# Seven block products in all four feed-forwards of a two-layer streaming encoder, with their additions on GpSimd

## What is computed

```python
for l in range(DEPTH):                       # 2 layers
    u = rmsnorm(x, norm1[l]) @ w_in[l]       # D_MODEL 1024 -> heads A, B and C
    # A: differential attention; B: attention over the best 256 (sample: 136) keys of an
    # index score per frame; C: gated linear recurrence; then one output projection
    x = x + merge_heads(...) @ w_out[l]
    a, gate = split(rmsnorm(x, norm2[l]) @ w_up[l])      # 1024 -> 2 x 2816
    conv = b_conv + sum(ext[:, j:j + t] * w_conv[j] for j in range(3))   # ext = history, a
    x = x + (silu(conv) * gate) @ w_down[l]
y = rmsnorm(x, final_norm)
```

## Time and profile before

| | us |
|---|---|
| median of 3 runs | 4004.64 |
| profiled execution | 4004.88 |
| its span | 4003.0 |
| TensorE busy | 3717.8 |
| VectorE busy | 2334.5 |
| ScalarE busy | 1125.3 |
| GpSimd busy | 758.4 |
| mean granted TensorE clock | 0.964 of full |

### The profile page before, as it was taken

How to read it: one execution, slowest core, us unless ns; L and a number is a source line. 1 busy time by engine, 2 the same in 40 slices (tenths; PEclk the granted TensorE clock), 3 DMA queues, 4 the chain that set the end, 5 groups by cost and what they waited for, 6 DMA issues and landing times. The chain is left out here.

```text
span 4003.0 us, 54393 instructions
## 1 busy us (share of the span) xinstructions
PE 3717.8 (93%) x21676; PEld 2953.6 (74%) x21676; DVE 2334.5 (58%) x4713; ACT 1125.3 (28%) x2668; POOL 758.4 (19%) x812
## 2 busy tenths in 40 slices
PE   7978899999999999999899989999899999899998
PEld 5755678777877777777667877787767777688887
DVE  1663556599964553549546454289955655544542
ACT  1123333211134442321334233111134443312221
POOL 2200121201001032221000014313010001353344
PEclk9988899999999999999999999999999999899999
DMA  4322233412222132342221213333221122242223
GB/s 141 96 76 75 81 98 89 129 67 70 79 67 68 51 96 93 90 124 89 62 91 54 80 59 96 115 110 122 70 69 52 42 75 69 70 149 83 65 89 96
DMA packets 152757, 339.54 MB, mean 85 GB/s; under 512 B 30312, under 2 KB 70824, under 8 KB 139192
## 3 DMA queue, kind: packets, MB, share of 16 engines
q1 hardware_dynamic: 92728, 291.04, 23.3%
q10 hardware_dynamic: 59776, 45.02, 3.9%
HBM read 299.33 MB, written 36.68 MB: 84 GB/s over the span
## 5 line engine op out<-in xcount | busy, mean ns | idle before, releaser
L835 PE MATMUL PS<-xn,wring 128*128 128x272 f32 (+1 forms) x7168 | 1709.1, 398 | 73.1 <-ACT dense L1163 29.2
L835 PEld LDWEIGHTS PS<-xn,wring 128*128 128x128 f32 x7168 | 1387.1, 196 | 348.1 <-issue 48.7
L1776 POOL TENSOR_TENSOR xT<-xT,res 128x272 f32<-128x272 f32 (+1 forms) x320 | 252.6, 790 | 2391.9 <-ACT res L1118 2356.6
L835 PE MATMUL PS<-dense,wring 128*128 128x256 f32 (+1 forms) x2816 | 666.1, 395 | 17.8 <-DVE dense L1436 9.2
L835 PEld LDWEIGHTS PS<-dense,wring 128*128 128x128 f32 x2816 | 541.6, 195 | 118.4 <-issue 10.7
L1545 DVE MAX8 top<-scr 128x8 f32<-128x384 f32 (+6 forms) x418 | 367.4, 879 | 12.5
L1546 DVE MATCH_REPLACE8 scr<-top,scr 128x384 f32<-128x384 f32 (+6 forms) x418 | 359.8, 861 | 0.0
L1118 ACT ACTIVATE res<-PS 128x272 f32<-128x272 f32 (+1 forms) x320 | 123.9, 389 | 600.5 <-PE PS L835 576.4
L856 PE MATMUL PS<-wring,xn 128*128 128x256 f32 (+1 forms) x1152 | 266.0, 391 | 3.7 <-ACT dense L1132 3.7
L856 PEld LDWEIGHTS PS<-wring,xn 128*128 128x128 f32 (+1 forms) x1152 | 213.3, 187 | 50.0 <-ACT dense L1132 5.4
L835 PE MATMUL PS<-catT,wring 128*128 128x272 f32 (+1 forms) x1024 | 231.1, 387 | 2.5 <-DVE catT L1615 1.8
(11 more groups left out here) (196 smaller groups left out, 4127.5 us busy)
## 6 DMA issues: line engine op xcount, KB each, us to landing
wring<-in_wu SPq DMA_DIRECT2D x88, 1024.0 KB, 4.8
wring<-in_wf SPq DMA_DIRECT2D x88, 512.0 KB, 3.8
wring<-in_wo SPq DMA_DIRECT2D x64, 512.0 KB, 3.7
wring<-in_wd SPq DMA_DIRECT2D x96, 320.0 KB, 2.9
wring<-in_wd SPq DMA_DIRECT2D x64, 384.0 KB, 3.1
wring<-in_wn SPq DMA_DIRECT2D x16, 1024.0 KB, 5.4
kv<-out_projT ACTq DMA_DIRECT2D x48, 256.0 KB, 4.1
out_projT<-dense SPq DMA_DIRECT2D x40, 272.0 KB
```

The costliest lines, as they stand in the source:

```text
L835: mm = nc.tensor.matmul(PS[:, dbank(t.g0), 0:cw], wtile(t.q, i), rhs, start=(kk == a), stop=(kk == b - 1))
L1776: nc.gpsimd.tensor_tensor(x, x, res[:, i % NRES, 0:cw], ALU.add).then_inc(s_res, 1)
```

## The change

`SEVEN` takes in n = 2 to 21 of F00, F01 and F10 too. There the additions of products stand in `add_products` and run on GpSimd; in F11 they stay on VectorE. The order of the products puts P7 ahead of P5. Weight sums are S3 = A11 - A21, S2 = A22 - S3, S1 = A21 + A22 and S4 = A12 - S2, made one by one between the additions: S2 in a new buffer `wsum`, S3 in `inv`, S1 and S4 in the ring's tile. T2, T3, T4 and the three parts p1, u2, u3 (now one set) lie in the columns of x that belong to the other half, T1 over B12 in `xn`. So x is stored half by half (`x_of`); SP puts the other half aside in the output y's memory beside P10 and P11 (`put_aside`) and loads it back in the last part of the down-projection (`load_again`; in F00 from the input), and GpSimd waits for that (`s_back`) before the next output projection. The first additions of the second half of a at 544 columns are cut at column 512 (`a_cols`). A pick is priced 1.3 times as high in the plan. x of the first half is loaded in eight whole transfers ahead of the first weight tile, and the norm of P01 stands in P01.

```diff
-SEVEN = {(1, 1): range(1, NF - 1)}
+SEVEN = {(0, 0): range(2, NF), (0, 1): range(2, NF), (1, 0): range(2, NF), (1, 1): range(1, NF - 1)}
-PRODUCTS = (Product("P1", "A11", "B11"), Product("P2", "A12", "B21"), Product("P6", "S2", "T2"), Product("P5", "S1", "T1"),
-            Product("P7", "S3", "T3"), Product("P3", "S4", "B22"), Product("P4", "A22", "T4"))
+PRODUCTS = (Product("P1", "A11", "B11"), Product("P2", "A12", "B21"), Product("P6", "S2", "T2"), Product("P7", "S3", "T3"),
+            Product("P5", "S1", "T1"), Product("P3", "S4", "B22"), Product("P4", "A22", "T4"))
+S_ORDER, T_ORDER = ("S3", "S2", "S1", "S4"), ("T3", "T2", "T4", "T1")
+U_ORDER = ("U2", "a0", "U3", "P5 + P3", "a1", "g0", "g1")
+ON_POOL = {(0, 0), (0, 1), (1, 0)}
...
-    if l == 0 and h == 0:
+    if l == 0:
         _norm(l, h, 0, 0, 1)
-    elif l == 0:
-        _turn("nsc", l, h, 0, 1, 0, ng=0)
     order = ((0, 0), (1, 0), (2, 0), (0, 1), (1, 1), (2, 1)) + tuple((n, j) for n in range(3, NPT) for j in range(2))
     done = 0
     for g, end, chunks in SECTIONS:
-        if (l, h, g) == (0, 0, "c"):
-            for j in range(2):
-                _root(0, 1, 0, j, 1)
         for n, j in order[2 * done:2 * end]:
             _turn("f", l, h, n, 0, j, load=("f", l, h, n, 0))
-            if (n, j) == (0, 0) and (l, h) == (0, 1):
-                _turn("nsc", l, h, 0, 1, 1, ng=0)
-            elif (n, j) == (0, 0):
+            if (n, j) == (0, 0):
                 _norm(l, h, 0, 1, 1 - l)
         for p in chunks:
...
             elif what == "pick":
-                out.append((0, 0, min(BURST, ROUNDS[h][y] - BURST * z) * 2 * (1.04 * k + 0.15), 0))
+                out.append((0, 0, min(BURST, ROUNDS[h][y] - BURST * z) * 2.6 * (1.04 * k + 0.15), 0))
...
+        wsum = sb("wsum", [P, 4 * P])
+        x_of = [x_all[h].rearrange("p (k t) -> p k t", k=KD) for h in range(2)]
...
+        def add_products(lane, eng, t):
+            (c0, cw), (c1, _) = GRP[t.h]
+            a, g, fixed = ab[:, t.n % 2, :], gb[:, t.n % 2, :], len(U_ORDER) * BLOCKS.index((t.l, t.h, t.n))
+            g0, g1 = g[:, c0:c0 + cw], g[:, c1:c1 + cw]
+            p1, u2, u3 = (part_of(t, i) for i in range(3))
+            name = PRODUCTS[t.p].name
+            def into_a(c, x, x0):
+                for b, w, gap in a_cols(t, c, cw):
+                    here = a[:, gap + b:gap + b + w]
+                    ins = eng.tensor_tensor(here, here, x[:, x0 + b - c:x0 + b - c + w], ALU.add)
+                ins.then_inc(s_fix, 1)
+            if name in ("P6", "P7", "P3", "P4"):
+                lane.wait_ge(s_ea, t.g0 + 1)
+            if name == "P6":
+                eng.tensor_tensor(u2, u2, p1, ALU.add).then_inc(s_fix, 1)
+                into_a(c0, p1, 0)
+            elif name == "P7":
+                lane.wait_ge(s_fix, fixed + 1)
+                eng.tensor_tensor(u3, u3, u2, ALU.add).then_inc(s_fix, 1)
+            elif name == "P3":
+                into_a(c1, g, c1)
+                lane.wait_ge(s_fix, fixed + 4)
+                into_a(c1, u2, 0)
+            elif name == "P4":
+                lane.wait_ge(s_fix, fixed + 4)
+                eng.tensor_tensor(g0, g0, u3, ALU.add).then_inc(s_fix, 1)
+                eng.tensor_tensor(g1, g1, u3, ALU.add).then_inc(s_fix, 1)
+        def tanh_turn(t, l, h, n):
+            k = UP_END[l, h, n]
+            return k + (3 if t.kind == "s" else 2 if TURNS[k].kind == "s" and t.p < 3 else 1)
+        def product_turn(t, l, h, n):
+            return tanh_turn(t, l, h, n) + (t.kind != "dn")
-            i = BLOCKS.index((t.l, t.h, t.n)) % 2
-            if name in ("S2", "S3", "S4"):
-                a = 1536 * i + 512 * int(name[1]) - 1024
-                return kv2[:, a:a + 512]
-            a = {"A11": 0, "A12": 512, "A21": 1024, "S1": 1024, "A22": 1536}[name]
+            if name in ("S2", "S3"):
+                return wsum[:] if name == "S2" else inv[:, 0:4 * P]
+            a = {"A11": 0, "A12": 512, "S4": 512, "A21": 1024, "S1": 1024, "A22": 1536}[name]
             return wring[:, t.q % NW, a:a + 512]
...
+            if name in ("T2", "T3", "T4") or name == "T1" and (l, h) == (1, 1):
+                a = 4 * cw * (int(name[1]) - 2)
+                flat = scr[:, 0:4 * cw] if name == "T1" else x_all[1 - h][:, a:a + 4 * cw]
+                return flat.rearrange("p (k t) -> p k t", k=4)
+            k, c = {"B11": (0, c0), "B12": (0, c1), "T1": (0, c1), "B21": (4, c0), "B22": (4, c1)}[name]
...
+            cw = GRP[t.h][0][1]
+            return x_all[1 - t.h][:, (12 + i) * cw:(13 + i) * cw]
...
             for k in range(KD):
-                sp.eng.dma_start(xT[:, k, 0:GMAX], io["xT"][k * P:(k + 1) * P, 0:GMAX]).then_inc(s_x[0][k], 16)
+                sp.eng.dma_start(x_of[0][:, k, :], io["xT"][k * P:(k + 1) * P, 0:W[0]]).then_inc(s_x[0][k], 16)
...
+            def put_aside(l, h):
+                z = max(k for k, t in enumerate(TURNS) if t.kind == "dn" and (t.l, t.h) == PROJS[PROJS.index((l, h)) - 1])
+                sp.wait_ge(s_res, ADDS[z] + 1)
+                sp.eng.dma_start(x_kept(1 - h), x_of[1 - h]).then_inc(s_aside, 16)
+            def load_again(l, h):
+                sp.wait_ge(s_mm, TURNS[UP_END[l, h, NF - 1]].g0 + 1)
+                sp.wait_ge(s_fix, len(U_ORDER) * sum(1 for x in BLOCKS if x[0:2] <= (l, h)))
+                if (l, h) in ASIDE:
+                    sp.wait_ge(s_aside, 16 * (ASIDE.index((l, h)) + 1))
+                src = x_kept(1 - h) if (l, h) in ASIDE else io["xT"].rearrange("(k p) t -> p k t", p=P)[:, :, C0[1 - h]:C0[1 - h] + W[1 - h]]
+                sp.eng.dma_start(x_of[1 - h], src).then_inc(s_back, 16)
+                for l, h in ASIDE:
+                    if k == STAGE[{(0, 1): "P10", (1, 0): "P11"}[l, h]][0] + 6:
+                        put_aside(l, h)
+                for l, h in BACK:
+                    if k == UP_END[l, h, NF - 1] + 10:
+                        load_again(l, h)
...
-                    if nextq == 0:
-                        for kk in range(KD):
-                            sp.eng.dma_start(xT[:, kk, GMAX:W[0]], io["xT"][kk * P:(kk + 1) * P, GMAX:W[0]]).then_inc(s_x[0][kk], 16)
...
+                    if name in ("P1", "P6", "P7"):
+                        act.wait_ge(s_xs, 4 * list(SEVEN).index((t.l, t.h)) + 1)
+                        act.wait_ge(s_fix, max(0, len(U_ORDER) * (B - 1) + {"P1": 2, "P6": 5, "P7": 7}[name]))
+                    else:
+                        act.wait_ge(s_h, max(0, U - 1))
...
-                if pending is not None and (t.kind == "dn" or k >= UP_END[pending[0:3]] + (4 if t.kind == "s" else 2)):
+                if pending is not None and k >= product_turn(t, *pending[0:3]):
...
+                    if (t.l, t.h) in SEVEN and (t.n, t.j) == (1, 1):
+                        b = lambda name: x_block(t.l, t.h, name)
+                        n0 = 4 * list(SEVEN).index((t.l, t.h))
+                        if (t.l, t.h) in ASIDE:
+                            dve.wait_ge(s_aside, 16 * (ASIDE.index((t.l, t.h)) + 1))
+                        dve.wait_ge(s_xn, KD * (SCALES.index(k) + 1))
+                        nc.vector.tensor_tensor(b("T3"), b("B22"), b("B12"), ALU.subtract).then_inc(s_xs, 1)
+                        dve.wait_ge(s_xs, n0 + 1)
+                        nc.vector.tensor_tensor(b("T2"), b("T3"), b("B11"), ALU.add).then_inc(s_xs, 1)
+                        dve.wait_ge(s_xs, n0 + 2)
+                        nc.vector.tensor_tensor(b("T4"), b("B21"), b("T2"), ALU.subtract).then_inc(s_xs, 1)
                 if t.kind == "s" and t.p == 0 and t.n == SEVEN[t.l, t.h][0]:
+                    b = lambda name: x_block(t.l, t.h, name)
+                    if (t.l, t.h) == (1, 1):
+                        dve.wait_ge(s_ct, NPAIR * 4)
+                    else:
+                        dve.wait_ge(s_mm, t.g0)
                     nc.vector.tensor_tensor(b("T1"), b("B12"), b("B11"), ALU.subtract).then_inc(s_xs, 1)
-                if t.kind == "s":
+                if t.kind == "s" and (t.l, t.h) not in ON_POOL:
+                    add_products(dve, nc.vector, t)
...
+            def weight_sum(B, name, x, y, op):
+                t = TURNS[LAST[("s",) + BLOCKS[B] + (0,)]]
+                i = 4 * B + S_ORDER.index(name)
+                pool.wait_ge(s_ws, i)
+                nc.gpsimd.tensor_tensor(w_block(t, name), w_block(t, x), w_block(t, y), op).then_inc(s_ws, 1)
+            def first_sums(B):
+                k = LAST[("s",) + BLOCKS[B] + (0,)]
+                weights_in(pool, TURNS[k].q)
+                pool.wait_ge(s_xn, KD * (norm_of(k) + 1))
+                if B:
+                    pool.wait_ge(s_mm, group_of(B - 1, "P7") + 1)
+                weight_sum(B, "S3", "A11", "A21", ALU.subtract)
+                weight_sum(B, "S2", "A22", "S3", ALU.subtract)
             for k, t in enumerate(TURNS):
-                if t.q + 1 in BLOCK_Q and k == FIRST_OF[t.q]:
```

(27 more changed lines are left out.)

108 lines of the change are left out of this document (39 added, 69 removed).

## The result

The kernel after takes 4037.6 us against 4012.5 of the kernel before, run beside it: ratio 1.0065, 95% interval [1.0045, 1.0085]. It is slower by 0.65%, 26 us; the forecast was 15 us faster, 3990. Its profiled execution has a span of 4034.6 us against 4003.0.

A forecast was written before the change was run, and what follows sets the result against it. VectorE was taken to bind where picks run, TensorE elsewhere. F00 with P10 lost 8 us, F01 won 10, F10 won 16 and reloads lost 3: 15 us off 4004.9, so 3990, range 3970 to 4012.

The forecast's parts named there:

- price of picks: Planner: picks weighing 1.3 times as much end later, giving F00's 373 us of dense time instead of 351.
- 3 for the reloads: SP's three loads of x back, queued ahead of weight tiles: 1 us each, 3 us lost in all.
- small edits: x by halves 0; P01's norm 0 (bounds -8 and +8); putting x aside 0; F11's sums 0 (-3 and +3).
- Outside them VectorE falls to 53% (1120 to 1453) and TensorE binds: Behind the picks: saved TensorE work counts there, less 10 us each in F01 and F10 (bounds 0 and 20).
- So the price falls on the two-input instructions: GpSimd lengthens only VectorE instructions with two SBUF inputs, five per block at 544 columns and four at 512.
- 0.38 us on five instructions: Lengthening per VectorE instruction (bounds 0 and 0.9): 1.9 us per block at 544 columns, 1.5 at 512.
- a sign of being wrong: Pick stretches: VectorE idle time there would mean a wait for GpSimd's a1 binds, or the gain is real.
- Picks don't suffer: One-input MAX8 keeps its time beside GpSimd: 0.828 us with GpSimd busy, 0.826 in F00.
- In the pick stretches VectorE is late anyway, so this costs nothing there: Convolution's wait for GpSimd's a1 and ScalarE's evictions' wait for its sums: no cost where picks run.
- Rival 1: GpSimd hinders VectorE much more, 0.9 us per hit on conv and product pairs: some 85 us, 4075; chance 0.31.
- discount that I took from the earlier trace: A VectorE hit costs up to 0.9 us, not a whole weight sum's 1.27, from L1510's 1.64 us in F11.
- 20 us by which I said it would shift the sum: With 1.27 us per hit, by the skill page, the total would come some 20 us later, at 4011.

The follow-up runs named there:

- c: Kernel after with product blocks in F11 alone, its plan price and small edits kept: 3943 us, ratio 0.9835 to the kernel before.
- e: Kernel before with one number changed, a pick priced at 2.6 instead of 2 in the plan: 3957 us, ratio 0.9866 to the kernel before.
- f: c plus useless GpSimd additions, as many and as wide as the new blocks' sums, nobody waiting for them: ratio 1.0056 to the kernel before.
- a: Kernel after with picks at their old price in the plan (2 instead of 2.6): ratio 1.0209 to the kernel before.
- b: Kernel after with the additions of products on VectorE in all stages, GpSimd keeping only the weight sums: ratio 1.0154 to the kernel before.
- p: Kernel after with VectorE making the sums into a1 itself in the three new stages: ratio 1.0066 to the kernel before.
- d: Kernel after with all GpSimd instructions of the new blocks on 8 columns, the rest of those sums left out: 3888 us, ratio 0.9701.
- j: c plus useless GpSimd additions only beside the blocks after the picks of F00, F01 and F10: ratio 0.9911 to the kernel before.
- r: Kernel after with each weight sum of the new blocks in four GpSimd instructions of 128 columns: 3983 us, ratio 0.9925 to the kernel before.
- q: Kernel after with each weight sum of the new blocks in two GpSimd instructions of 256 columns: 4012 us, ratio 1.0002 to the kernel before.
- m: Kernel after with the new blocks' weight sums on 8 columns, their rest left out, activation sums whole: 3937 us, ratio 0.9808.

## Why the prediction was wrong

**Where the sum failed.** The recorded sum mixes two causes, which c and e separate. Its terms for the price of picks are +25, +8 and +9 us in the three stretches of picks, 51, 18 and 26 us less dense time behind them, and 6 for the mixers: about -47. Measured alone (e), the price gives -54. Its terms for the product blocks are +35, +14 and +17 us where picks run and -57 + 20 behind them, so +29; with 3 for the reloads that makes the -15. Measured against c, which has the same plan, the blocks cost 92: the stretches of picks grow by 38, 16 and 9 us (63, against 66), and the stretches behind them by 4, 25 and 0 us (+29, against -37). The small edits, put at nothing, gave -12.

The step that failed is therefore "Outside them VectorE falls to 53% (1120 to 1453) and TensorE binds", with 57 us of TensorE work counted as gained there and 0, 10 and 10 us allowed for the blocks' price. It is 66 us off, more than the whole miss of 41 (26 measured, -15 forecast).

**TensorE's work.** 480 instructions fewer and 107 us of work at full pace: the count is right. But between c and the kernel after, which differ in these blocks alone, TensorE's busy time falls by 31 us (3699 to 3669) and its idle time grows by 132.
```profile
2117.21 1.89 PE L914 MATMUL PS<-xn,wring 128*128 128x256 f32 x8
...
2124.97 0.49 PE L992 MATMUL PS<-kv 32*128 32x128 f32 x4 [0.79 <-ACT scr L1338]
...
2127.70 0.20 PE L1019 MATMUL PS<-ident,scr 32*32 32x32 f32 x1 [0.60 <-ACT scr L1350]
2127.83 3.67 PE L914 MATMUL PS<-xT,inv 128*128 128x256 f32 x8
```

and the granted clock there (the column before the last two):

```profile
2117.20:2119.10 1.90, 1.90 (x11) 1.40 (x11) 0.78 (x1) 0.38 (x1) 1.82 (x3) 1.00 0.33 63
2127.80:2131.40 3.60, 3.60 (x9) 2.52 (x8) 2.08 (x4) 0.87 (x5) 0.00 (x0) 0.53 0.00 0
```

The sum had no term for it. f, with c's matmuls unchanged, has 62 us more idle time and 34 more busy time, so waits and a lower clock came together there too. The rate isn't fixed: a has 53 us more idle and 11 more busy time than the kernel after, and b 46 more idle and 26 less busy time, at a higher clock (0.959 against 0.953).

**VectorE's additions and the pick stretches.** Right in length, wrong in the list and in the state of the engines, so in part by luck. Forecast for the stretches 385, 140 and 176 us (371 by 0.96 is 387), measured 397, 147 and 186. "So the price falls on the two-input instructions" fails: the conv pair got off lightly (L1568 and L1569 0.797 and 0.888 us for 546 columns against 0.788 in c, not 1.1), and the copies of 2 columns, not in the sum at all, took 82 us where in c they take 37 (L1560 to L1565); the one-input L1567 went from 0.566 to 0.709. The forecast's 0.38 us on five instructions happened to give nearly the right total. In F00's picks VectorE was to be busy for over 95% and TensorE for about 85%; both are at 91%, VectorE has 360 us of work and not 371, and 37 us of idle time, which the prediction had named as a sign of being wrong. "Picks don't suffer" is right to the digit.

**Hand-overs.** "In the pick stretches VectorE is late anyway, so this costs nothing there", said of the convolution's wait for a1 and of "ScalarE's evictions for its sums", is the second term that failed. Moving a1 to VectorE (p) indeed gains nothing, but TensorE's block products wait for evictions. TensorE's longest waits in the kernel after:

```profile
PE PS L914 <- ACT xT L1216: 42.6, 24, 6.2
PE PS L1019 <- DVE scr L1651: 41.5, 23, 5.1
PE PS L914 <- ACT dense L1213: 26.5, 11, 7.9
PE PS L1019 <- DVE scr L1644: 26.5, 23, 4.8
...
PE PS L914 <- ACT dense L1216: 22.2, 8, 5.3
```

The three of L914 are those of block products, 91 us of the 132, and 60 of them lie where picks run; in c L914 runs in F11 alone and doesn't stand among the longest. The two of mixers were there before: 26.2 and 23.7 us in c. What held ScalarE each time was not taken apart: with short sums (d) the three come to 35 us, and in F00's picks ScalarE's tanh itself waits 54 us for VectorE's convolution, 35 in c.

**Outside the picks.** By stage, c and the kernel after (F00, F01, F10 of each):

```profile
725.00:1416.00 691.00, 674.68 (x3315) 525.50 (x3316) 501.46 (x918) 192.36 (x430) 104.85 (x137) 0.99 0.25 80
1725.00:2414.00 689.00, 656.80 (x4256) 526.12 (x4255) 438.58 (x1057) 220.88 (x579) 101.09 (x134) 0.98 0.27 86
2640.00:3436.00 796.00, 745.57 (x4609) 571.62 (x4608) 530.12 (x1000) 264.39 (x568) 109.85 (x136) 0.97 0.23 71
```
```profile
733.00:1447.00 714.00, 652.14 (x3097) 498.94 (x3097) 535.85 (x905) 207.53 (x478) 325.40 (x395) 0.96 0.25 80
1775.00:2505.00 730.00, 649.56 (x4096) 510.61 (x4095) 506.76 (x1060) 242.02 (x640) 316.37 (x355) 0.94 0.27 84
2732.00:3537.00 805.00, 724.99 (x4449) 545.00 (x4448) 586.21 (x993) 282.26 (x628) 336.73 (x396) 0.95 0.23 73
```

VectorE gains 68 us of work in F01 and 56 in F10, most of it behind the picks (53 and 44), and TensorE's idle time rises from 16 to 62, 32 to 80 and 50 to 80 us: by 71 us where picks run and by 57 behind them. A share of 53% is a mean; j shows that VectorE's added work costs there all the same, 30 us for 110. That leaves about 56 us behind the picks (the 29 measured, the 57 of TensorE work that brought nothing, less 30). Block products waiting for evictions are 32 us of it, the clock stands beside them (0.93 to 0.96 against 0.97 to 0.98), and no run separates the two.

**The plan.** Its effect on where the picks end came out right (last pick 397 us into F00's up-projections, 385 forecast). I entered it only as dense time moved from one stretch to the other, and never asked what it gives without the products. It is 54 us, by which the kernel came close to even: without it the kernel is 2.1% slower than before (a).

**Small edits.** Costed at nothing; with P01's norm in P01, x in tiles and F11's order they gave 12 us, 5 of them in F11. No run separates the rest.

**The cases.** Rival 1 named the direction, the instruments and "about 1 us in each of the 32 other blocks"; it put the conv pair in the place of the copies, and its 4075 was 37 us too far (its parts add up to 101 us and not 85, so 4091). What it lacked is that the price depends on GpSimd's longest instruction. The discount that I took from the earlier trace rows was a misreading. L1510 starts there 0.59 us after the weight sum shown has ended; what it met is the next one:

```profile
3716.69 1.59 POOL L1770 TENSOR_TENSOR wring<-wring 128x512 f32<-128x512 f32 x1
```

Of its 1.64 us, 1.08 pass before that weight sum ends. The Trainium skill's rule (the section of "SBUF — State Buffer" named in the prediction: whoever comes second waits for the whole instruction) is borne out: the copy above waits out 1.19 us, all that was left of a weight sum of 1.27 us. The 20 us by which I said it would shift the sum were the right sign.

## What to carry to other kernels

In these runs, work moved to GpSimd beside a busy VectorE was priced by the length of its single instructions and by what each VectorE instruction costs while it waits, down to copies of 2 columns: keep reading GpSimd instructions short (here 128 columns for 512 gave back 56 us with 12% more GpSimd work), and don't let one event release both a short VectorE instruction and a long GpSimd one. Saved TensorE work is worth its full time only if TensorE doesn't wait more: count the new waits, and the clock that can fall with them. When a change comes with a new constant in a planner, price the constant by itself, as it may be the larger effect.

## What the hardware showed unexpectedly

- A VectorE copy of 2 fp32 columns lasts 0.15 to 0.19 us on average without GpSimd's block work and up to 1.28 us when GpSimd is reading; MAX8 of 640 columns keeps its 0.827 us.
- 708 us of GpSimd additions that nobody waits for cost the kernel 89 us; 274 us of memsets, with the same count and widths, 7 us, which is within the scatter.
- Between c and the kernel after, 143 us more at the lower clock, 129 of them with TensorE busy, took back about 65 of 107 us of saved TensorE work.
- A GpSimd weight sum of 128 columns took 0.50 to 0.55 us, of 256 columns 0.76 to 0.85, of 512 1.33 to 1.41 (means by buffer in r, q and the kernel after), and of 8 columns 0.28 to 0.32 (d and m); the shortest additions of 8 columns took 0.22 (d). So 0.2 to 0.3 us of each don't shrink with the width, more than the 0.18 by which I had reckoned from the earlier trace rows.
